# Moving the weight-residue subtraction of units 36 to 195 from GpSimd to VectorE in a float32 encoder-trunk kernel

## The reference, cut to what matters

```python
def shortconv_mixer(h, buf, w_in, conv_w, w_out):
    bg, cg, u = jnp.split(h @ w_in, 3, axis=-1)
    y, new_buf = causal_dwconv(cg * u, buf, conv_w)
    return (bg * y) @ w_out, new_buf

def conv_ffn(h, buf, w_up, conv_w, conv_b, w_down):
    z = h @ w_up
    zc, new_buf = causal_dwconv(z, buf, conv_w)
    gate, up = jnp.split(zc + conv_b, 2, axis=-1)
    return (jax.nn.silu(gate) * up) @ w_down, new_buf

for i in range(2):
    x = x + mixer_i(rmsnorm(x, norm_mix[i]))      # GLA, then shortconv
    x = x + conv_ffn(rmsnorm(x, norm_ffn[i]))
return rmsnorm(x, norm_final), ...
```

## Time and profile before

| | us |
|---|---|
| median of three runs | 1628.05 |
| span of the profiled execution | 1624.3 |
| its own time beside the span | not given; the median is 3.75 above the span |
| TensorE matmul busy | 1547.9 (95%) |
| VectorE busy | 1058.9 (65%) |
| GpSimd busy | 512.5 (32%), of it 485.9 in the subtractions `wl` |
| ScalarE busy | 458.6 (28%) |
| mean granted clock of TensorE | 0.984 |

### The profile page before, as it was taken

One profiled execution on the slowest core, in us unless ns is written; L12 is line 12 of the kernel. 1 busy time (PEld: TensorE's weight loads), 2 busy tenths in 40 slices (PEclk: granted clock), 3 DMA queues, 4 the chain that ended last, 5 costly groups with the idle time before them and its releaser, 6 DMA issues.

```text
span 1624.3 us, 26037 instructions
## 1 busy us (share of the span) xinstructions
PE 1547.9 (95%) x10292; PEld 1522.0 (94%) x10292; DVE 1058.9 (65%) x1313; ACT 458.6 (28%) x717; POOL 512.5 (32%) x221
## 2 busy tenths in 40 slices
PE   6999999999999999999998999998999999999995
PEld 5999998899999999999998999998999999999994
DVE  6556665755956666666767553368966666667667
ACT  4345664443212121212115111115211111121123
POOL 4322220243323333233233333333333323332331
PEclk8999999999999999999999999999999999999997
DMA  5211116222222222221222222212122222222211
GB/s 205 70 61 53 53 53 229 102 66 66 69 70 70 78 65 66 76 76 54 77 78 71 80 68 78 74 59 78 54 77 78 65 77 65 77 64 65 78 37 65
DMA packets 34873, 123.76 MB, mean 76 GB/s; under 512 B 3920, under 2 KB 6864, under 8 KB 33648
## 3 DMA queue, kind: packets, MB, share of 16 engines
q1 hardware_dynamic: 31872, 108.37, 21.2%
q10 hardware_dynamic: 2928, 14.35, 2.3%
HBM read 114.48 MB, written 8.22 MB: 76 GB/s over the span
## 4 chain that ended last, share of the span: by engine, by line
PE 74%; DVE 17%; DVEq 4%; issue 2%; ACT 1%; DMA 0%; POOL 0%; SPq 0%; ACTq 0%
PE ps L401 58%; PE ps L417 8%; DVE hh L972 4%; DVE x L761 3%; DVE y L965 2%; DVE y L961 2%; PE ps L484 2%; PE ps L584 2%; DVEq L1017 1%; DVE sq L728 1%; DVE xl L712 1%; DVEq L1002 1%; PE ps L536 1%; PE ps L691 1%; DVE zp L984 1%
## 5 line engine op out<-in xcount | busy, mean ns | idle before, releaser
L345 POOL TENSOR_TENSOR wl<-raw,wh 128x1024 fp32r<-128x1024 f32 x195 | 485.9, 2498 | 1003.1 <-ACT wh L1173 1003.1
L401 PE MATMUL ps<-xh,wh 128*128 128x328 f32 (+5 forms) x2176 | 506.5, 314 | 15.6 <-DVE xl L712 15.3
L401 PE MATMUL ps<-xl,wh 128*128 128x328 f32 (+5 forms) x2176 | 503.1, 313 | 0.0
L401 PE MATMUL ps<-xh,wl 128*128 128x328 f32 (+5 forms) x2176 | 502.7, 313 | 0.0
L401 PEld LDWEIGHTS ps<-xh,wh 128*128 128x128 f32 x2176 | 389.3, 190 | 18.8 <-issue 9.5
L401 PEld LDWEIGHTS ps<-xl,wh 128*128 128x128 f32 x2176 | 390.2, 190 | 0.0
L401 PEld LDWEIGHTS ps<-xh,wl 128*128 128x128 f32 x2176 | 389.5, 190 | 0.0
L1173 ACT ACTIVATE wh<-raw 128x1024 fp32r<-128x1024 f32 x196 | 204.3, 1055 | 346.6 <-PE ps L401 323.3
L417 PE MATMUL ps<-gh,wh 128*128 128x322 f32 (+1 forms) x800 | 186.3, 314 | 30.3 <-DVE x L761 30.2
L965 DVE SCALAR_TENSOR_TENSOR y<-zp,par,y 128x660 f32<-128x660 f32 (+1 forms) x192 | 185.6, 967 | 26.9 <-issue 22.1
L761 DVE TENSOR_TENSOR x<-ps,x 128x644 f32<-128x644 f32 (+2 forms) x208 | 161.7, 821 | 53.8 <-PE ps L417 28.7
(11 more groups left out here) (154 smaller groups left out, 1153.4 us busy)
## 6 DMA issues: line engine op xcount, KB each, us to landing
raw<-w_units SPq DMA_DIRECT2D x196, 512.0 KB, 3.5
s<-states ACTq DMA_DIRECT2D x4, 1024.0 KB, 5.3
state_sample<-snew ACTq DMA_DIRECT2D x4, 1024.0 KB, 4.1
x<-x_t SPq DMA_DIRECT2D x8, 328.0 KB, 6.5
x<-x_t ACTq DMA_DIRECT2D x1, 2624.0 KB, 11.4
y_t<-x SPq DMA_DIRECT2D x6, 320.0 KB, 2.4
ffn_last<-zl ACTq DMA_DIRECT2D x2, 396.0 KB, 2.4
zc<-ffn_cache ACTq DMA_DIRECT2D x1, 704.0 KB, 4.2
```

Of the source, the lines that this page charges most:

```text
L345: pool.tensor_tensor(wl[:, j, :, :], raw[:, j, :, :], wh[:, j, :, :].bitcast(F32), ALU.subtract).then_inc(sem["lo_done"], 1)
L401: mm = pe.matmul(ps[:, p, c:c + z - a], w[:, ring, k, :], v[:, k, a:z], start=(k == 0 and w is wh and v is hi), stop=(k == KT - 1 and w is ...
```

## The change

From unit 36 on (`BY_POOL`), VectorE does the subtraction and signals `more_lo_done`. It is issued at hand-picked places of VectorE's program: one after each z unit, one after additions m = 1 and m = 5 of each down pair, two in `update_x` for n = 2 and 3 (after addition m = 1 and after the last `xl`), and three after each half group of the mixer, each call for the unit three further on than the one counted. GpSimd's loop is shortened, SP and TensorE wait for the semaphore that belongs to the unit.

```diff
+BY_POOL = 2 * HEADS + 16 + 8 + RING
@@ sync
-        with sp.Fori(0, N_UNITS // RING - 1) as i:
+        with sp.Fori(0, BY_POOL // RING) as i:
             for j in range(RING):
                 sp.wait_ge(sem["lo_done"], RING * i + j + 1)
                 sp.dma_start(raw[:, j, :, :], w_in[bass.ds(RING * i + (RING + j), 1)]
                              .rearrange("u p m n -> p (u m) n")).then_inc(landed[j], 16)
+        with sp.Fori(BY_POOL // RING, N_UNITS // RING - 1) as i:
+            for j in range(RING):
+                sp.wait_ge(sem["more_lo_done"], RING * i + (j + 1 - BY_POOL))
                 sp.dma_start(raw[:, j, :, :], w_in[bass.ds(RING * i + (RING + j), 1)]
                              .rearrange("u p m n -> p (u m) n")).then_inc(landed[j], 16)
@@ gpsimd
-        with pool.Fori(0, N_UNITS // RING - 1 - before_out) as i:
+        with pool.Fori(0, BY_POOL // RING - 1 - before_out) as i:
@@ tensor
+        def weights(unit, i=0):
+
+            if unit < BY_POOL:
+                pe.wait_ge(sem["lo_done"], unit + 1)
+            else:
+                pe.wait_ge(sem["more_lo_done"], 12 * i + (unit + 1 - BY_POOL))
...
-            weights(n_ready)
+            weights(unit, i)
@@ tensor, project_down
-            weights(n_ready)
+            weights(unit + 1, i)
@@ vector, update_x
                 add_to_x(p, m, first)
+                if n > 1 and m == 1:
+                    low()
...
             split_low(n, KT - 1)
+            if n > 1:
+                low()
@@ vector
+        unit = 2 * HEADS + 16 + 8
+
+        def low(n=1, i=0):
+
+            nonlocal unit
+            for _ in range(n):
+                u, unit = unit + RING - 1, unit + 1
+                if u < BY_POOL or u >= N_UNITS:
+                    continue
+                j = u % RING
+                dve.wait_ge(sem["hi_done"], 12 * i + (u + 1))
+                dve.tensor_tensor(wl[:, j, :, :], raw[:, j, :, :], wh[:, j, :, :].bitcast(F32),
+                                  ALU.subtract).then_inc(sem["more_lo_done"], 1)
+
@@ vector, group
                 z_unit(("z", layer, g, j), layer, z0 + j, j, i)
+                low(1, i)
                 if j == 1 or j == 3 and not late:
                     gate_z(layer, g, j, f_count)
@@ vector, down
                 add_to_x(take(("down", layer, g, m), i), m, FIRST_Z[layer] + STEP)
+                if m in (1, 5):
+                    low(1, i)
@@ vector, mixer
                         if e == 0 or g == 0:
                             gate_mix(E)
+                        low(3)
...
                         add_to_x(take(("mix_out", g - 1, m)), m, FIRST_MIX)
+                        if m in (1, 5):
+                            low()
@@ vector, after the loop of a layer
+            unit += 12 * (TRIPS - 1)
```

More of the change, by code:

```diff
@@ L258, in build @@
     ps = nc.alloc_psum_tensor("ps", [P, RING, 2 * BANK], F32)
-    names = ["par_in", "more_par_in", "gla_in", "wgd_done", "hi_done", "lo_done", "units_used", "consts",
+    names = ["par_in", "more_par_in", "gla_in", "wgd_done", "hi_done", "lo_done", "more_lo_done", "units_used", "consts",
              "xs_hi", "xs_lo", "sq_done", "pool_sq_done", "sum_done", "log_done", "root_done", "soft_done", "mask_in", "d_done", "e_done",
@@ L325, in _ @@
             sp.dma_start(raw[:, j, :, :], w_in[j]).then_inc(landed[j], 16)
-        with sp.Fori(0, N_UNITS // RING - 1) as i:
+        with sp.Fori(0, BY_POOL // RING) as i:
             for j in range(RING):
                 sp.wait_ge(sem["lo_done"], RING * i + j + 1)
+                sp.dma_start(raw[:, j, :, :], w_in[bass.ds(RING * i + (RING + j), 1)]
+                             .rearrange("u p m n -> p (u m) n")).then_inc(landed[j], 16)
+        with sp.Fori(BY_POOL // RING, N_UNITS // RING - 1) as i:
+            for j in range(RING):
+                sp.wait_ge(sem["more_lo_done"], RING * i + (j + 1 - BY_POOL))
                 sp.dma_start(raw[:, j, :, :], w_in[bass.ds(RING * i + (RING + j), 1)]
@@ L387, in copied, with project @@
             pe.wait_ge(freed[p], n + 1)
-        def weights(n_ready):
-            pe.wait_ge(sem["lo_done"], n_ready)
-        def project(step, hi, lo, n_ready, ring, first=0, cut=HALF, i=0, release=1, before=None):
+        def weights(unit, i=0):
[3 more added lines that the diff above has]
+                pe.wait_ge(sem["more_lo_done"], 12 * i + (unit + 1 - BY_POOL))
+        def project(step, hi, lo, unit, ring, first=0, cut=HALF, i=0, release=1, before=None):
             p = open_slot(step, i)
-            weights(n_ready)
+            weights(unit, i)
             for k in range(KT):
@@ L406, in project, with project_down @@
             mm.then_inc(filled[p], 1)
-        def project_down(step, first, f0, n_ready, rings, i=0, release=1, g_count=None):
-            weights(n_ready)
+        def project_down(step, first, f0, unit, rings, i=0, release=1, g_count=None):
+            weights(unit + 1, i)
             pe.wait_ge(sem["g_done"], g_count)
@@ L444, in _ @@
             for j, kind in enumerate("kq"):
-                project((kind, h), xh, xl, n_unit + 1, n_unit % RING, release=1 if n_unit else 0,
+                project((kind, h), xh, xl, n_unit, n_unit % RING, release=1 if n_unit else 0,
                         before=(x_ready(0), norm_amid(0))[j] if h == 0 else None)
@@ L502, in value @@
             nonlocal n_unit
-            project((kind, h, e), xh, xl, n_unit + 1, n_unit % RING)
+            project((kind, h, e), xh, xl, n_unit, n_unit % RING)
             n_unit += 1
@@ L601, in _ @@
             p = open_slot(("w_out", m))
-            weights(n_unit + m + 1)
+            weights(n_unit + m)
             for k in range(KT - 2):
@@ L624, in _ @@
         for m in range(EARLY, KT):
-            project(("w_out", m), oh, ol, n_unit + 1, n_unit % RING, FIRST_ATT, middle(FIRST_ATT))
+            project(("w_out", m), oh, ol, n_unit, n_unit % RING, FIRST_ATT, middle(FIRST_ATT))
             n_unit += 1
@@ L633, in _ @@
                     for j in range(6):
-                        project(("mix", g, j), xh, xl, n_unit + 1, n_unit % RING, FIRST_MIX, middle(FIRST_MIX),
+                        project(("mix", g, j), xh, xl, n_unit, n_unit % RING, FIRST_MIX, middle(FIRST_MIX),
                                 release=2 if j == 0 and (g != 1) else 1,
@@ L638, in _ @@
                     if g:
-                        project_down(lambda m, g=g: ("mix_out", g - 1, m), FIRST_MIX, 2 * ((g - 1) % 2), n_unit + 2,
+                        project_down(lambda m, g=g: ("mix_out", g - 1, m), FIRST_MIX, 2 * ((g - 1) % 2), n_unit,
                                      [n_unit % RING, (n_unit + 1) % RING], g_count=g_before + 2 * g)
                         n_unit += 2
-                project_down(lambda m: ("mix_out", MIX_G - 1, m), FIRST_MIX, 2 * ((MIX_G - 1) % 2), n_unit + 2,
+                project_down(lambda m: ("mix_out", MIX_G - 1, m), FIRST_MIX, 2 * ((MIX_G - 1) % 2), n_unit,
                              [n_unit % RING, (n_unit + 1) % RING], release=2, g_count=g_before + 2 * MIX_G)
@@ L650, in z_units @@
                     u = n_unit + j
-                    project(("z", layer, g, j), xh, xl, 12 * i + (u + 1), u % RING, FIRST_Z[layer],
+                    project(("z", layer, g, j), xh, xl, u, u % RING, FIRST_Z[layer],
                             middle(FIRST_Z[layer], PROMPT), i=i,
@@ L659, in down_units @@
                 u = n_unit
-                project_down(lambda m: ("down", layer, g, m), FIRST_Z[layer] + STEP, 2 * (g % 2), 12 * i + (u + 2),
+                project_down(lambda m: ("down", layer, g, m), FIRST_Z[layer] + STEP, 2 * (g % 2), u,
                              [u % RING, (u + 1) % RING], i=i, release=release, g_count=count)
@@ L682, in last_norm @@
             pe.matmul(bank(p, c), ones[:, :], sq[:, 0, half(c)], start=True, stop=True).then_inc(filled[p], 1)
-        weights(N_UNITS)
+        weights(N_UNITS - 1)
         pe.wait_ge(sem["g_done"], g_before)
```

## The result

| | before | after |
|---|---|---|
| median (lowest to highest, 4 runs each) | 1626.82 (1623.06 to 1630.64) | 1662.87 (1658.53 to 1664.43) |
| span of the profiled execution | 1624.3 | 1662.2 |
| its own time | not given | 1664.43 |
| mean granted clock of TensorE | 0.984 | 0.972 |

The changed kernel is slower: 1.0223 times the time of before, 95% interval 1.0198 to 1.0248, 36 us by the medians. The prediction was 1669 us in a range of 1643 to 1692 us. Whether it is slower by 2%, which the prediction gave 0.87, stays open, because the interval reaches across 1.02; that it is slower is clear.

What follows compares the result with a forecast made beforehand. TensorE was taken as the busy engine, waiting on VectorE's queue order. 1624.3 - 19.8 (FFN halves) + 56.4 (mixer waits) + 16 (clock) - 11.4 (norms) = 1665.5 us, with 3.75 us to the median 1669 us; range 1643 to 1692 us.

Steps and rivals of the forecast that it cites:

- What bounds the kernel: Whole kernel: TensorE busy 1547.9 of 1624.3 us; VectorE's place in the queue, not its busy sum, is the bound.
- The price of a subtraction: VectorE's queue: each of 160 added subtractions lasts 1.23 us and takes 1.15 us of the queue, 184 us in all.
- The blocking: Ahead of addition m = 2 in an FFN half: GpSimd holds VectorE up for 3.4 us, which goes.
- The mixer: Mixer half groups: eight new waits for late subtractions, five of 7.5 and three of 6.3 us, 56.4 us lost.
- The clock: Behind the mixer's eight new waits: TensorE's clock falls, 2.0 us lost each, 16 us (bounds 0 and 24).
- The norms: Norms of mixer and second FFN: waits fall to 1.5 us, clock holds, 11.4 us gained (bounds 0 and 15).
- The sum: Whole kernel: gains and losses give a span of 1665.5 us, plus 3.75 us to the median, 1669 us; chance 0.84.
- FFN halves: FFN down pairs: addition m = 2 comes 1.1 us earlier, 18 times, 19.8 us gained (bounds 5 and 30).
- B: Mixer: TensorE never waits there and only the gains are left, 1597 us; chance 0.09.
- C: FFN halves: GpSimd does not cause the long instructions, each of 18 halves loses 2.3 us, 1730 us; chance 0.03.
- D: Whole kernel: neither engine of the change is the busy one, so time stays at 1628 us; chance 0.04.

Runs made afterwards that it cites:

- The doubled one: The subtraction behind addition 1 of each FFN down pair done twice, against the kernel with one subtraction after each mixer unit: 1621.82 us, one run.
- The first experiment: The mixer's three subtractions issued one after each unit, against the changed kernel: 1592.04 us, 0.9772 of before.

## Why the prediction was right

**What bounds the kernel.** Right: TensorE does, and what counts is which instruction of VectorE it waits for. The 65% of VectorE stayed 65%.

**The price of a subtraction.** Predicted 1.23 us, measured 1.22 (1212 to 1226 ns over 160). The doubled one cost 1.29 us with its drain.

**The blocking.** Predicted 3.4 us ahead of addition 2, and it was all given back: m = 2 came 1.2 us earlier, and a half is 1.1 to 1.2 us shorter (1.1 predicted). In the list of waits it is 30.2 - 8.3 = 21.9 us against 19.8. The sum had no term for the clock there: it fell behind two of the waits before (24 matmuls in 5.38 and 5.31 us in the chain, where the others took 3.8) and behind none after, another 3.0 us. The blocking itself was read from two overlaps in one half; the run with idle work on GpSimd is what shows it as a cause.

**The mixer.** Right in place, number and size: eight waits, at units 101, 104, 107, 115 and 123 and at the three down pairs, 7.36 and 5.94 us against 7.5 and 6.3 reckoned, 54.6 against 56.4 us. The excess lies mostly in the 0.3 us that I had added to each for TensorE to be in step again: from the end of the subtraction to the first matmul it is 0.1 to 0.2 us. At the down pairs the convolution was 0.1 us shorter, too.

**The clock.** Predicted 2.0 us a wait, measured 2.05 to 2.8, in sum 19.6 against 16 us. The 2.0 was a choice below the 2.7 us that the rows of a norm's wait of 4.88 us allowed; the rows did not fix it.

**The norms.** Predicted a wait of 1.5 us each, measured 1.17, and the clock held; 7.5 us of waiting and 4 us of slow matmuls are gone, 11.5 us against 11.4:

```profile
868.19 1.34 PE L439 MATMUL ps<-sq,ones 128*128 128x328 f32 x4 [1.17 <-DVE sq L738]
```

**The sum.** By terms, predicted and measured: FFN halves -19.8 and -24.9, the mixer's waits +56.4 and +54.6, the clock there +16 and +19.6, norms -11.4 and -11.5. That is +41.2 predicted and +37.8 by these readings; the three stages differ by 37.3 us together, the spans by 37.9, the medians by 36.0. The errors of the terms (5.1 us too little gained, 1.8 too much waiting, 3.6 too little for the clock) partly cancel, which is luck, but each is small beside the 56 us that decide. They explain half of the 6 us between 1669 and 1663 us. The other half comes from the 3.75 us that I added between span and median: after the change the median is only 0.7 us above the profiled span. The first experiment confirms the split: with the mixer's waits gone, 36.5 us are gained on before by stage, where I had 31.

**The rivals.** B (only the gains, 1597 us) described what happens once the mixer's order is mended, which measured 1592 us; for the change as made it failed on the ground given, that the subtractions are queued behind the take of the third unit. C (the long instructions are not GpSimd's doing) fell with the idle work that brought them back. D fell: losses and gains didn't cancel. Of the two rules of the Trainium skill cited for it, the first was read too far: TensorE was the engine to improve, but it does not follow that a change on two others has no effect. The order of VectorE, 65% busy, decided 74 us one way, and its relief from GpSimd 37 us the other. The second (moving between the two may not help as they share a read port) holds in its reason and not in its conclusion, as the move ended the contention: with the calls in good order it is worth 38 us.

## What to carry to other kernels

Where an engine in order serves the one that bounds, count for each wait which of its instructions stands ahead of the signal. A hand-placed "n units ahead" must be checked at every place where calls are bunched: three calls after the third unit are none ahead for the first of them. A move that takes work from GpSimd can pay for itself on VectorE, because two-input instructions there stop waiting (194 us added, 29 us more busy here); but put the moved work behind whatever TensorE is waiting for, not ahead of it.

## What the runs showed of the hardware that I had not expected

A GpSimd instruction with SBUF inputs (1.90 us) beside VectorE cost 93 us over 160 of them, one that only writes (0.95 us) nothing that one run can show. The clock is not settled by the length of the wait. It fell behind all waits for `wl` of 4.9 to 7.4 us (eight in the changed kernel, eight with the subtractions ahead of the gate, two beside the idle work), behind four of eight of 2.27 and 3.32 us, behind 13 of 16 of about 2 us beside the idle work, behind five of 20 of 1.7 us on average, behind two of the 18 of that mean before, and behind none of those of 0.5 us. Those 16 stand each in a down pair that itself began behind a wait of 0.3 to 0.65 us for `wl`, which the down pairs of the other kernels did not; whether that matters no run here separates. Each fall cost 1.5 to 2.9 us.
